# A hybrid decoder layer whose experts are computed densely: 64 of 256 tokens take their picked expert rows instead

## The reference

```python
def peer(h, w_query, sub_keys, expert_u, expert_v):
    q = (t @ w_query).reshape(n_tok, 8, 2, 64)
    s = jnp.einsum('thcd,hcnd->thcn', q, sub_keys)
    v1, i1 = lax.top_k(s[:, :, 0], 16)
    v2, i2 = lax.top_k(s[:, :, 1], 16)
    cand = (v1[..., :, None] + v2[..., None, :]).reshape(n_tok, 8, 256)
    best, j = lax.top_k(cand, 16)
    e_idx = take(i1, j // 16) * 128 + take(i2, j % 16)
    gate = jax.nn.softmax(best, axis=-1)
    ...
    u_sel = expert_u[ec]
    a = jax.nn.gelu(jnp.einsum('cd,chkd->chk', tc, u_sel), approximate=False)
    w = gc * a
    return jnp.einsum('chk,chkd->cd', w, expert_v[ec])
```

## Time and profile before

| | us |
|---|---|
| median of 3 runs | 2296.4 (2295.87 to 2296.57) |
| profiled execution | 2295.72 |
| its span, first to last instruction | 2293.9 |
| busy: PE, DVE, ACT, POOL | 2255.6, 1367.1, 1109.2, 592.3 |
| HBM read, written | 417.22 MB, 21.10 MB |
| TensorE's granted clock, mean | 0.996 of 2.4 GHz |

### The profile page before, as it was taken

One profiled execution on the slowest core, in us unless ns is written; L12 is line 12 of the kernel. 1 busy time (PEld: TensorE's weight loads), 2 busy tenths in 40 slices (PEclk: granted clock), 3 DMA queues, 4 the chain that ended last, 5 costly groups with the idle time before them and its releaser, 6 DMA issues.

```text
span 2293.9 us, 44271 instructions
## 1 busy us (share of the span) xinstructions
PE 2255.6 (98%) x15624; PEld 2099.1 (92%) x15624; DVE 1367.1 (60%) x2195; ACT 1109.2 (48%) x1570; POOL 592.3 (26%) x285
## 2 busy tenths in 40 slices
PE   6999999999999899999999999999999999999998
PEld 5999999999999899999999999999888888888887
DVE  6666655666664547877775444444555555555555
ACT  5555555555653435656564333334444444444443
POOL 1000000000000005888888888860000000000000
PEclk9999999999999999999999999999999999999999
DMA  5545555555455356767776666665666666666666
GB/s 197 190 170 185 192 194 189 161 173 185 157 174 179 129 184 181 180 184 182 183 183 183 183 183 181 181 183 198 217 216 217 215 217 215 217 216 218 217 218 221
DMA packets 171222, 438.69 MB, mean 191 GB/s; under 512 B 51904, under 2 KB 68416, under 8 KB 171072
## 3 DMA queue, kind: packets, MB, share of 16 engines
q1 hardware_dynamic: 129456, 419.37, 54.0%
q0 software_dynamic: 41600, 16.94, 6.5%
q10 hardware_dynamic: 144, 2.10, 0.2%
HBM read 417.22 MB, written 21.10 MB: 191 GB/s over the span
## 4 chain that ended last, share of the span: by engine, by line
PE 97%; DVE 2%; ACT 0%; DMA 0%; issue 0%; DVEq 0%; SPq 0%; ACTq 0%
PE psum L419 21%; PE psum L424 21%; PE psum L420 21%; PE psum L610 20%; PE psum L616 10%; PE psum L528 0%; PE psum L527 0%; PE psum L496 0%; PE psum L487 0%; PE psum L495 0%; PE psum L586 0%; DMA arena<-x_t 0%; PE psum L450 0%; PE psum L550 0%; DVE small L892 0%; DVE arena L907 0%
## 5 line engine op out<-in xcount | busy, mean ns | idle before, releaser
L346 DVE TENSOR_TENSOR wlo<-raw,whi 128x1024 fp32r<-128x1024 f32 x752 | 920.6, 1225 | 803.7 <-PE psum L424 505.9
L419 PE MATMUL psum<-xr,whi 128*128 128x256 f32 (+1 forms) x3968 | 991.0, 287 | 10.1 <-DVE xr L1034 8.5
L420 PE MATMUL psum<-xr,whi 128*128 128x256 f32 (+1 forms) x3968 | 981.0, 284 | 0.0
L339 ACT ACTIVATE whi<-raw 128x1024 fp32r<-128x1024 f32 x752 | 756.5, 1050 | 83.4 <-PE psum L424 47.4
L419 PEld LDWEIGHTS psum<-xr,whi 128*128 128x128 f32 x3968 | 760.1, 192 | 12.9 <-issue 7.7
L420 PEld LDWEIGHTS psum<-xr,whi 128*128 128x128 f32 x3968 | 760.8, 192 | 1.0
L879 POOL DMA_INDIRECT gates<-xr x256 | 570.5, 2228 | 440.1 <-DVE xr L1163 361.7
L424 PE MATMUL psum<-xr,wlo 128*128 128x256 f32 (+1 forms) x3968 | 559.1, 283 | 1.6 <-DVE wlo L346 1.6
L424 PEld LDWEIGHTS psum<-xr,wlo 128*128 128x128 f32 x3968 | 513.3, 191 | 1.9 <-DVE wlo L346 1.8
L610 PE MATMUL psum<-whi,xr 128*128 128x512 f32 x2048 | 505.8, 389 | 0.0
L610 PEld LDWEIGHTS psum<-whi,xr 128*128 128x128 f32 x2048 | 384.4, 188 | 79.7
(11 more groups left out here) (198 smaller groups left out, 888.4 us busy)
## 6 DMA issues: line engine op xcount, KB each, us to landing
raw<-stream SPq DMA_DIRECT2D x752, 512.0 KB
gates<-arena POOLq DMA_DIRECT2D x8, 2048.0 KB, 12.5
small<-gates SPq DMA_DIRECT2D x128, 128.0 KB, 3.0
gates<-xr POOLq DMA_INDIRECT x256
arena<-x_t SPq DMA_DIRECT2D x4, 544.0 KB, 6.8
h_rows<-arena ACTq DMA_DIRECT2D x1, 2048.0 KB, 9.8
raw<-h_rows SPq DMA_DIRECT2D x4, 512.0 KB, 4.2
out<-arena SPq DMA_DIRECT2D x8, 256.0 KB, 3.1
```

Source lines behind the costliest of these rows:

```text
L339: nc.scalar.activation(whi[:, s * HALF:(s + 1) * HALF], raw[:, s * HALF:(s + 1) * HALF], ACT.Copy).then_inc(hi_done, 1)
L346: nc.vector.tensor_tensor(wlo[:, k % 2 * HALF:(k % 2 + 1) * HALF], raw[:, s * HALF:(s + 1) * HALF], f(whi[:, s * HALF:(s + 1) * HALF]), AL ...
L419: mm(acc, w, hi[c], start=start and c == 0, stop=False)
L420: mm(acc, w, lo[c], start=False, stop=False)
```

## The change

Tokens 0 to 191 (`TD`) stay dense. The last 64 (`TS`) take only their picks.

- The dense parts shrink from 256 to 192 tokens: `W`, the table of gates (`gates_at`, now 128 x 128 x 192) and the moving side in U. `expert_half` multiplies `whi` with hi and lo tokens side by side (384 columns, 8 instructions) and `wlo` with the hi tokens (192 columns, 8 instructions). ACT copies the lo part out of PSUM, DVE adds the hi part, and then Gelu runs in place. In V a half has 10 products instead of 12: for the second tile, 64 tokens wide, the hi and lo weights lie side by side (`Wboth`), so one pair of products serves both.
- The 64 tokens lie on 128 partitions, each token twice, with 64 of its 128 picks on either (`ROWS` = 64). GpSimd gathers for each of 64 picks a row of `u_rows` (128 rows of 2048 elements, an indirect DMA) into a ring of three slots (`got`). DVE multiplies a row with the token's and sums (`row_product`), ACT takes the Gelu of the 64 dots, DVE multiplies in the gates, and for 64 rows of `v_rows` DVE adds the scaled row to an accumulator (`row_sum`). Both are one DVE instruction over 2048 elements a row. The 128 rows are spread over the halves from 30 to 496 of the 512 of U and V, one for each 3.67 halves (`row_at`).
- Routing: the turns now take 13 halves instead of 8 (`route_at`), and the second tile comes first. One reduction of 512 elements takes the place of two of 256 and their combination, with one small product more.
- GpSimd's queue: in U, 60 gathers and 192 scatters (128 for the first tile, 64 for the dense half of the second), interleaved by hand: heads 0 to 6 have eight groups of a gather, one scatter of the second tile and (from head 1) two of the first; head 7 has four groups of a gather and ten scatters; then gathers alone. Gather n waits until row n - 3 is used.
- SP waits at half 244 of U until all scatters have landed, and then loads the first gates. The moves of picks between partitions (`move_picks`) are DMAs of SP.
- `expert_v` is now read from `v_rows` by halves of rows. DVE's, ACT's and SP's loops in U and V are partly written out without loops.
- Ahead of U, 16 transposes make rows of the 64 tokens. At the end the 64 rows are moved between partitions, summed and stored, and the second tile's dense rows take a hop between partitions.

```diff
+TD = 192
+TS = T - TD
+NS = TOPK // 2
+ROWS = HEADS * NS
+RING = 3
...
+        TURN = 13
+        def route_at(t, m):
+            return (t * 8 + m) * TURN // 8
+        def row_at(s):
+            return 2 * TURN + 4 + s * (4 * NK - 12 - 2 * TURN - 4) // (2 * ROWS)
...
+            for m in range(2 * B_U):
+                k = 2 * F_U + m
                 sp.wait_ge(lo_done, k + 1)
-                load(k + 4, k % 4)
+                if k + 4 < 2 * F_V:
+                    load(k + 4, k % 4)
+                else:
+                    load_v((k + 4 - 2 * F_V) // 2, k % 2, k % 4)
+                for h in range(HEADS):
+                    if m == route_at(2 * h, 7) + 3:
+                        move_picks(h)
+                if m == 2 * B_U - 12:
+                    sp.wait_ge(scattered[0], 16 * NSEL)
+                    sp.wait_ge(scattered[1], 16 * ROWS)
+                    for n in range(2):
+                        load_gates(n, n)
...
+            def expert_half(base, k, q, j):
+                s = k % 4
+                pe.wait_ge(hi_done, base + k + 1)
+                for c in range(8):
+                    mm(bank(2 + q, 0, 2 * TD), whi[:, s * HALF + c * P:s * HALF + (c + 1) * P], y[:, 8 * j + c, :, 0:TD],
+                       start=j == 0 and c == 0, stop=False)
+                pe.wait_ge(lo_done, base + k + 1)
+                s = k % 2
+                for c in range(8):
+                    last = mm(bank(2 + q, 0, TD), wlo[:, s * HALF + c * P:s * HALF + (c + 1) * P], y[:, 8 * j + c, 0, 0:TD],
+                              start=False, stop=j == 1 and c == 7)
+                last.then_inc(half_done, 1)
...
+                    hi_w, lo_w = whi[:, s * HALF:(s + 1) * HALF], wlo[:, s2 * HALF:(s2 + 1) * HALF]
+                    part(0, psum, Whi[c % 2][:, 0:P], hi_w, first, False)
+                    pe.wait_ge(w_lo, w_base + c + 1)
+                    part(0, psum, Wlo[c % 2][:, 0:P], hi_w, False, False)
+                    part(1, psum, Wboth[c % 2], hi_w, first, False)
                     pe.wait_ge(lo_done, base + k + 1)
+                    part(1, psum[0:TS, :], Whi[c % 2][:, P:TD], lo_w, False, True)
+                    last = part(0, psum, Whi[c % 2][:, 0:P], lo_w, False, True)
...
+            def gather(n):
+                s = n % RING
+                if n >= RING:
+                    pool.wait_ge(row_used, n - RING + 1)
+                h, table = n % ROWS, (u_rows, v_rows)[n // ROWS]
+                pool.indirect_dma_start(got[s], None, table,
+                                        bass.IndirectOffsetOnAxis(sparse_row[:, h:h + 1].bitcast(U32), 0)
+                                        ).then_inc(row_in[s], 16)
...
             for h in range(HEADS):
+                pool.wait_ge(moved[h % 2], 64 * (h // 2 + 1))
+                for m in range(NS):
+                    gather(h * NS + m)
+                    if h < HEADS - 1:
+                        scatter_rest(h, m)
+                        if h:
+                            for k in (2 * m, 2 * m + 1):
+                                scatter_first(h - 1, k)
+                    elif m < 4:
+                        for k in (2 * m, 2 * m + 1):
+                            scatter_rest(h, k)
+                        for k in range(m % 2 * NS, (m % 2 + 1) * NS):
+                            scatter_first(h - 1 + m // 2, k)
+            for n in range(ROWS, 2 * ROWS):
+                gather(n)
...
+            def row_product(n):
+                s = n % RING
+                if n == 0:
+                    dve.wait_ge(x_rows_twice, 16)
+                dve.wait_ge(row_in[s], 16 * (n // RING + 1))
+                V.tensor_tensor_reduce(out=got[s], in0=got[s], in1=x_rows, scale=1.0, scalar=0.0, op0=ALU.mult,
+                                       op1=ALU.add, accum_out=dots[:, n:n + 1]).then_inc(row_used, 1)
+            def row_sum(n):
+                s, k = n % RING, n - ROWS
...
+                dve.wait_ge(row_in[s], 16 * (n // RING + 1))
+                dve.wait_ge(row_used, n)
+                V.scalar_tensor_tensor(acc, got[s], dots[:, k:k + 1], acc, ALU.mult, ALU.add).then_inc(row_used, 1)
...
+            for n in range(B_U):
+                for j in range(2):
+                    m = 2 * n + j
+                    late_half(m)
+                    if j:
+                        dve.wait_ge(low_part, n + 1)
+                        V.tensor_tensor(W[:, n, :], bank(2 + n % 2, 0, TD), W[:, n, :], ALU.add).then_inc(bank_free, 1)
+                    if m in (2 * B_U - 6, 2 * B_U - 5):
+                        gate_weights(m - (2 * B_U - 6))
+                    step(m)
+            for q in range(2):
+                weight_lo(q)
+            for c in range(B_V - 2):
+                m = 2 * B_U + 2 * c
+                late_half(m)
+                gate_weights(c + 2)
+                step(m)
+                late_half(m + 1)
+                weight_lo(c + 2)
+                step(m + 1)
```

More of the change, by code:

```diff
@@ L576, in _ @@
                 mul_block(2 * F_QUERY, 2 * q, F_QUERY + q + 1, bank(q, 0, T), hi, lo, None if q else 15)
+            pe.wait_ge(rows_act, 2)
+            for k in range(KC):
+                last = nc.tensor.transpose(bank(2, k * P, P), h2[:, k, P:T], C["ident"])
+            last.then_inc(x_rows_ps, 1)
             with pe.Fori(0, B_QUERY // 2 - 1) as i:
@@ L821, in expert_blocks @@
-            def expert_blocks(first, last):
-                with act.Fori(first // 4, last // 4) as i:
-                    for q in range(4):
-                        expert_block(i * 8 + 2 * F_U, i, q)
-                        for j in range(2):
-                            hi_half(act, i * 8 + 2 * F_U, 2 * q + 4 + j)
-            expert_blocks(B_U // 2, 3 * B_U // 4)
-            act.wait_ge(picked, 2 * HEADS)
-            act.wait_ge(rows_out, 16)
-            expert_blocks(3 * B_U // 4, B_U - 4)
@@ new lines, in _ @@
+            for n in range(B_U):
+                if n == 0:
+                    route_helps(0)
+                act.wait_ge(half_done, 2 * F_U + 2 * n + 2)
+                if n == B_U - 2:
+                    act.wait_ge(scattered[0], 16 * NSEL)
+                    act.wait_ge(scattered[1], 16 * ROWS)
+                A(one_weight(n), bank(2 + n % 2, TD, TD), ACT.Copy).then_inc(low_part, 1)
+                for j in range(2):
+                    hi_half(act, 0, 2 * F_U + 2 * n + 4 + j)
+                if n:
+                    gelu(n - 1)
+                    route_helps(n)
+                if n == B_U - 1:
+                    gelu(n)
@@ L835, in weight_hi @@
             def weight_hi(chunk, q):
                 act.wait_ge(scaled, chunk + 1)
[L837 to L845 removed]
+                A(Whi[q], one_weight(chunk), ACT.Copy)
@@ new lines, in scatter, with scatter_first @@
+            def scatter(b, at, gate):
+                pool.indirect_dma_start(every, bass.IndirectOffsetOnAxis(at.bitcast(U32), 0), gate, None,
+                                        compute_op=ALU.add).then_inc(scattered[b], 16)
+            def scatter_first(h, k):
+                if k == 0:
+                    pool.wait_ge(picked[0], h + 1)
+                    if h:
+                        pool.wait_ge(scattered[0], 16 * TOPK * h)
+                n = h * TOPK + k
+                scatter(0, pick_at[:, n:n + 1], pick_gate[:, n:n + 1])
@@ L1196, in _ @@
[L1196 to L1210 removed]
+            ch.spare = small[:, 1046:1078]
@@ new lines, in weight_lo @@
+            def weight_lo(chunk):
+                q = chunk % 2
+                dve.wait_ge(w_hi, chunk + 1)
+                V.tensor_tensor(Wlo[q], W[:, chunk, :], f(Whi[q]), ALU.subtract).then_inc(w_lo, 1)
+            for n in range(B_U):
+                for j in range(2):
+                    m = 2 * n + j
[6 more added lines that the diff above has]
+                    step(m)
@@ L1213, in lay_out @@
+            for j in range(2):
+                half = slice(j * HALF, (j + 1) * HALF)
+                dve.wait_ge(tail_moved[j], 16)
+                dve.wait_ge(res_sb, j + 1)
+                V.tensor_tensor(res[0:TS, half], res[0:TS, half], low[0:TS, half], ALU.add).then_inc(out_sb, 1)
 def lay_out(inputs):
```

438 lines of the change are left out of this document (244 added, 194 removed).

## The result

The changed kernel takes 2482.0 us (median, 2479.2 to 2487.9), the kernel before 2296.1 us beside it: a ratio of 1.081 (95% interval 1.079 to 1.083). The forecast of 2197 us had the sign wrong, and its range did not hold the time.

The account below looks back on a forecast made before the run. The prediction took TensorE, 98% busy at 2.4 GHz, to bound the kernel before. Its terms, 852 + 2 + 734 (U) + 595 (V) + 11, gave a 2194 us span and a forecast of 2197 us, range 2110 to 2330 us.

Parts of the forecast that it names:

- ahead of U: Stages before U: 852 us as profiled, plus 2 us for 16 new transposes.
- tail: End of the span: 6.7 us as before, plus three passes of 1024 elements and a partition hop, 11 us.
- 116 + 236 x 2.83 + 28: Upper end of U, with GpSimd launches at 2.83 us each; the prediction gave 807 us.
- Rival (c): In U, 192-column products cost TensorE plain float32's rate, 0.40 us each: whole 2635 us; chance 0.12.
- a half with a row keeps DVE for up to 4.9 us, and the slack is two halves, so single stalls are short; I add nothing for them: VectorE in U: stalls from picked rows priced at nothing, beside a pace of 2.66 us per half.
- the same list of operations: VectorE's routing in U: 9.9 us per turn kept, spread over 13 halves instead of 8.
- rival (b): GpSimd launches get longer: from 2.95 us on slower than before, at 3.2 us the whole 2362 us; chance 0.15.
- (a): GpSimd launches seldom meet two-input instructions, 1.85 us each: U 687 us, the whole 2150 us; chance 0.15.
- Covered, as long as rows arrive: In V, VectorE's work of 2.05 us per half stays under TensorE's 2.27 us.
- with 93% of the better rate in use I expect some late loads: V transfers need 537 us at 398 GB/s, beside 580 on TensorE; V taken as 595 us.
- My own marker: Stated sign of being wrong: V halves that exceed 2.5 us.
- rival (d): Transfers bound V at 339 GB/s: V 630 us, the whole 2232 us; chance 0.10.

Follow-up runs that it names:

- exp1: The changed kernel with ScalarE's exponential one block (two halves) earlier in its order: 2426.5 us.
- all3_slim: all3 with all gathers except the first three of each table fetching 128 columns of a row instead of 2048: V 593 us, U 700 us.
- all3: The changed kernel with the edits of gates4 and exp1, and the first tile's scatters in their own head's groups: 2226.5 us, ratio 0.969 to the kernel before.
- gates4: The changed kernel with four buffers for gates instead of two, their loads two blocks earlier: 2310.7 us.
- order: The changed kernel, still two gate buffers, with the gates' load in V issued ahead of a lo_half wait and table load on SyncE: 2355.0 us.
- no_rows: The changed kernel without gathers, row products and row sums, so the last 64 tokens lack their picks: 2148.0 us.
- all3_thin: all3 with VectorE's row product and row sum cut to 64 of 2048 columns, transfers whole: U 665 us, V 617 us.
- all3_tail: all3 with the accumulator's move and a load of residual rows issued five blocks before the end of V: 2219.6 us, ratio 0.966.
- late: all3_tail with SyncE's wait for all scatters at half 249 of U instead of 244: 2208.1 us, ratio 0.961.

## Why the prediction was wrong

Its sum by its own terms, against after:

| term | predicted | measured |
|---|---|---|
| ahead of U | 852 + 2 | 853.7 |
| U | 734 (703 to 807) | 806 |
| V | 595 (580 to 630) | 795 |
| tail | 11 | 25 |
| span | 2194 | 2479.6 |

The 807 us at the upper end of U are 5 us too few by the prediction's own terms: 116 + 236 x 2.83 + 28 is 812. It changes neither the forecast nor the range.

**TensorE: right.** Timeline of after, where nothing is late; three rows of U, then three of V:

```profile
1503.29 1.59 PE L679 MATMUL psum<-xr,whi 128*128 128x384 f32 x8
1504.72 1.03 PE L684 MATMUL psum<-xr,wlo 128*128 128x192 f32 x8
1505.58 1.59 PE L679 MATMUL psum<-xr,whi 128*128 128x384 f32 x8
...
1669.23 1.54 PE L704 MATMUL psum<-whi,xr 128*128 128x512 f32 x6
1670.61 1.08 PE L704 MATMUL psum<-wlo,xr 128*64 128x512 f32 x4
1671.53 1.54 PE L704 MATMUL psum<-whi,xr 128*128 128x512 f32 x6
```

A U half is 2.29 us (2.27 predicted): 1.43 us for eight products of 384 columns, 179 ns each, and 0.86 us for eight of 192, 108 ns each. A V half is 2.30 us (2.27). Rival (c), plain float32's rate at 192 columns, fell with the 108 ns.

**VectorE's instructions: right; its pace in U: wrong, since its waits stood at nothing.** Row product 2.29 us (2.32), row sum 2.35 (2.38), new sum 0.35 recorded. But from row 0 to row 48, 176 halves, it took 551.8 us in after (938.5 to 1490.3), 3.14 us a half, not 2.66, and row 0 itself came 85 us into U, not 68. VectorE was busy for 452.3 us of that stretch, 2.57 us a half, so its work was priced rightly. But that is 82% of the time, not over 90%: the rest are waits. The step that failed is "a half with a row keeps DVE for up to 4.9 us, and the slack is two halves, so single stalls are short; I add nothing for them", and ahead of it "the same list of operations": the list is the same, but it stands among other halves, and I never placed ScalarE's exponential against the piece that waits for it. exp1 shows that part: 2.83 us a half (929.8 to 1427.1). There VectorE is busy for 452.1 us, as before, so what is left over the forecast, 0.17 us a half or 30 us, is not work but waits too: 14.2 us still for the exponential, and 17.2 ahead of the first piece of a turn (line 1269), where the program waits for ScalarE's copy of the scores (line 919); at 1101.77 us that piece began 0.04 us behind the end of that copy. Late loads have a part as well (U is 25 us shorter in all3_slim than in all3).

**GpSimd: the launches too dear, their role too large.** In after a scatter took 1.9 us and a gather of `u_rows` 1.5 on average, with 0.3 between; a group of head 7 took about 22 us, not 27.5. Launches of GpSimd:

```profile
L1002 POOL DMA_INDIRECT gates<-arena x128: 1542/1756/3498, 999.8 to 1622.9; - x128
```

With the pause that is some 2.1 us a launch, where I took 2.5. That a launch is held up by VectorE's instructions with two inputs is borne out: of the 192 scatters in after, the 50 that began while VectorE ran nothing took 1.54 to 1.57 us, the 84 that began under a lo_half 2.04 on average, and the 21 under a row product 2.56, up to 3.50. But in the second stretch of the earlier trace rows 107 of the 111 launches began under a lo_half, where the 2.83 us came from, and in after fewer than half of them did. So the price stayed under mine: rival (b) with 2.95 and more fell, and (a) with 1.85 was nearer on the price, but its time of 2150 us was not. Heads 1 to 6 were paced by VectorE, as (a) has it. The end of U went as the text says: late rows (25.8 us of waits), SyncE at half 244, a stop of TensorE for 34.8 us. From row 48 to the end of U it is 170 us, where the forecast had 193. So U was forecast about 95 us too short up to row 48 and 23 too long behind it, 72 too short in all; exp1 gives 62 of the 72 back.

**V: the failed step that decided the sign.** "Covered, as long as rows arrive" checked VectorE's busy time, and "with 93% of the better rate in use I expect some late loads" checked the bytes. Neither asks when each small load is issued, what stands ahead of it, and what stands behind the instruction that waits for it. The gates' landing time of 3.0 us stood in the page of before as a fact of that kernel; with 67 MB of rows on the same 16 DMA engines it became 6.7. gates4 takes 171 of the 186 us by which after is slower than before; order shows the part of the late issue, and no_rows and all3_slim the part of the rows. My own marker, V halves over 2.5 us, came true (3.10).

**Transfers: rival (d) was right, one layer down.** Once the gates are out of the way, V runs at 337 to 344 GB/s at a share of 0.93 to 0.94, and takes 617 to 633 us over gates4, all3, all3_thin, all3_tail and late, against 630 by (d) and 595 in the forecast. The 398 GB/s of the earlier trace rows, twelve microseconds of plain loads with nothing else going on, are not a rate that this mixture held. The Trainium skill (DMA: Bandwidth & Descriptors, Specifications) puts the limit of HBM for one core at some 358 GB/s, and its section on bandwidth has 425 GB/s for a single core with its neighbour idle. V's rates lie under the first and nearest to it, but the 398 of the earlier trace rows lie above it and under the second. So the runs do not show which limit holds in V, and why 340 and not 398 was not tested.

**Tail.** I had priced three passes of 1024 elements, 3.7 us. Two of them are of 2048 (lines 1384 and 1386, 2.29 us each) and one is done in two parts (line 1400, 2.3 us together), 3.2 us more than I took; and the wait for the accumulator's move, 11.1 us behind queued loads, was missing. all3_tail took the wait out. The two make up the error of 14 us.

The late kernel is the same design with five places in the order of its queues mended. It takes 2208 us: the design is worth 4%, and the five places cost 12%. That the forecast of 2197 lies near it is partly luck, since its U was 23 us longer and its V 38 us shorter than in that kernel.

## What to carry to other kernels

Work that moves from a busy engine to idle ones adds transfers and longer lists to in-order queues: for every wait in a loop, work out the time from issue to use, with the landing time stretched (here 3.0 to 6.7 us), and not only the load of each engine. When the profile of a result shows no engine and no transfer near its limit (here 85% at most), look for a loop through a load, in the chain: the period of the repeated pieces gives the price, and one more buffer or two swapped lines mend it. An instruction placed by block on one engine and by half on another must be compared in time after every change of the schedule.

## What the runs showed of the hardware

- Float32r products of 192 columns took 108 ns each when one weight load of 128 columns stood before each; by the slope of the earlier trace rows the columns alone would be 94. That the weight load sets this floor fits the 108 ns that the prediction worked out of the earlier trace rows; no run varied the load.
- A gather of 128 rows of 8 KB, 1 MB, occupied GpSimd's queue for 1.50 us on average from `u_rows` (0.94 to 1.94) and 1.72 from `v_rows` (1.49 to 3.35), no more than a scatter of 128 single words (1.9 on average, 1.54 to 3.50). From `v_rows` it landed in 8.5 us.
- The same 96 KB load landed in 4.4 us at a DMA share of 0.74 without the gathers, in 4.5 at 0.77 with as many gathers of a sixteenth of the bytes (all3_slim), and in 6.7 at 0.75 with gathers of 1 MB. The share alone does not tell the latency; the size of the transfers beside it did.
- ScalarE's load of a table took 1.28 us with every exponential (the row at 1121.24). The Trainium skill (ScalarE: Activation LUTs, What ACT_TABLE_LOAD costs) gives about 1283 ns for the load, and the trace agrees. The drain of some 1380 ns that it adds does not show: the exponential at 1122.54 began 0.02 us behind the load.
- The kernels with gathers spread more: all3 ran in 2217.6 to 2233.5 us and after in 2479.2 to 2487.9, the kernel before in 2295.4 to 2298.0. Why was not tested.
